# Spilled gate matrices laid out in DRAM by partition and group of four expert rows

## The reference

```
act  = einsum('thkd,td->thk', u_tab[experts], h)
coef = gates * gelu(act)
out  = einsum('thk,thkd->td', coef, v_tab[experts])
```

## Time and profile before

| | us |
|---|---|
| median of 3 runs | 2995.08 |
| lowest and highest run | 2994.76 and 2996.53 |
| span of the profiled execution, first to last instruction | 2994.5 |
| TensorE busy in that span | 2935.5 |

### The profile page before, as it was taken

The page is one execution under the profiler, slowest core; times in us unless marked ns, Lnnn a source line. Parts: engine busy times, 40 slices in busy tenths (PEclk is TensorE's granted clock), DMA queues, the critical chain, the costliest instruction groups (busy, mean ns, idle before and its releaser), DMA issues.

```text
span 2994.5 us, 49015 instructions
## 1 busy us (share of the span) xinstructions
PE 2935.5 (98%) x17798; PEld 2756.1 (92%) x17798; DVE 2529.9 (84%) x4848; ACT 1471.7 (49%) x2353; POOL 955.4 (32%) x709
## 2 busy tenths in 40 slices
PE   7999999999999999999999999999999999999998
PEld 4777799999999999999977778999999999999998
DVE  4667799989896899899886779998989868988988
ACT  3354234488884333333343532446888733333333
POOL 0000036545453333233300000655545433333331
PEclk9999999999999999999999999999999999999999
DMA  7425646799999999999931122569999899999996
GB/s 277 176 99 209 248 132 208 264 342 372 354 352 360 347 357 362 358 355 362 361 104 64 64 72 86 178 200 335 365 383 366 308 380 351 359 365 354 354 364 233
DMA packets 252363, 836.79 MB, mean 279 GB/s; under 512 B 24640, under 2 KB 57664, under 8 KB 241472
## 3 DMA queue, kind: packets, MB, share of 16 engines
q1 hardware_dynamic: 158336, 453.50, 42.5%
q0 software_dynamic: 89280, 348.17, 31.6%
q10 hardware_dynamic: 4608, 33.56, 2.7%
HBM read 751.24 MB, written 83.89 MB: 279 GB/s over the span
## 4 chain that ended last, share of the span: by engine, by line
PE 86%; DVE 5%; DMA 4%; ACT 2%; issue 1%; POOL 0%; SPq 0%; DVEq 0%; ACTq 0%; POOLq 0%
PE banks L998 41%; PE banks L1511 31%; PE banks L1479 5%; DMA w_raw<-wst 2%; PE banks L1319 2%; DVE w_lo L1552 1%; PE banks L1063 1%; PE banks L1014 1%; DMA ring<-u,gidx 1%; ACT w_hi L712 1%; PE banks L1402 1%; DMA pj<-adaw 1%; DVE vacc L2051 1%; PE banks L1493 0%; PE banks L1160 0%
## 5 line engine op out<-in xcount | busy, mean ns | idle before, releaser
L712 ACT ACTIVATE w_hi<-w_raw 128x1024 fp32r<-128x1024 f32 x596 | 631.7, 1060 | 813.1 <-PE banks L998 636.9
L1552 DVE TENSOR_TENSOR w_lo<-w_raw,w_hi 128x1024 fp32r<-128x1024 f32 x522 | 639.3, 1225 | 345.2 <-ACT w_hi L712 335.5
L998 PE MATMUL banks<-hH,w_hi 128*128 128x368 f32 (+1 forms) x2528 | 881.5, 349 | 5.5 <-ACT w_hi L712 2.4
L998 PE MATMUL banks<-hH,w_lo 128*128 128x368 f32 (+1 forms) x2528 | 861.1, 341 | 0.0
L998 PE MATMUL banks<-hL,w_hi 128*128 128x368 f32 (+1 forms) x2528 | 860.6, 340 | 0.0
L1511 PE MATMUL banks<-c_hi,w_hi 128*128 128x368 f32 x2048 | 675.8, 330 | 2.1 <-DVE w_lo L1552 2.1
L1511 PE MATMUL banks<-c_lo,w_hi 128*128 128x368 f32 x2048 | 674.3, 329 | 0.0
L1511 PE MATMUL banks<-c_hi,w_lo 128*128 128x368 f32 x2048 | 673.0, 329 | 0.0
L676 POOL DMA_INDIRECT ring<-u,gidx x288 | 420.9, 1461 | 451.6 <-DVE gact L2039 417.6
L676 POOL DMA_INDIRECT ring<-v,gidx x288 | 330.6, 1148 | 695.7 <-DVE vacc L2051 635.9
L998 PEld LDWEIGHTS banks<-hH,w_hi 128*128 128x128 f32 x2528 | 475.3, 188 | 50.5 <-issue 18.6
(11 more groups left out here) (323 smaller groups left out, 2966.3 us busy)
## 6 DMA issues: line engine op xcount, KB each, us to landing
w_raw<-wst SPq DMA_DIRECT2D x596, 512.0 KB
activations<-act_out SPq DMA_DIRECT2D x128, 368.0 KB
act_in<-activations SPq DMA_DIRECT2D x64, 736.0 KB
gate_matrices<-stage ACTq DMA_DIRECT2D x32, 1024.0 KB
gates<-gate_matrices SPq DMA_DIRECT2D x64, 512.0 KB
ada_buf<-adaw POOLq DMA_DIRECT2D x24, 1024.0 KB, 7.0
nrm<-adaw POOLq DMA_DIRECT2D x8, 1024.0 KB, 5.3
pj<-adaw POOLq DMA_DIRECT2D x7, 1024.0 KB, 7.1
```

The source lines that it names most:

```text
L712: nc.scalar.activation(w_hi[g % 2][:, :, :].rearrange("p a b -> p (a b)"), w_raw[:, g % RAWS, :], ACT.Copy).then_inc(s_wh, 1)
L998: last = mm(bank[s][:, 0:t.stop - t.start], a[s][:, k, :], b[:, k, t], start=(k == 0 and a is w_hi and b is hH), stop=(k == KT - 1 and a i ...
L1552: v.tensor_tensor(w_lo[g % 2][:, :, :].rearrange("p a b -> p (a b)"), w_raw[:, g % RAWS, :], w_hi[g % 2][:, :, :].rearrange("p a b -> p (a ...
```

## The change

The DRAM tensor `gate_matrices` had the order chunk, partition, row, token. It gets the order partition, group of four rows, chunk, row in the group, token. The same bytes are stored and loaded, by the same 32 stores and 64 loads, at the same places of each engine's program, behind the same waits. What differs is how long a run of neighbouring bytes in DRAM is for each partition.

- A load of a group's gates (512 KB) took for each partition four runs of 1 KB, one from each chunk, 4 MB apart, and the partitions lay 32 KB apart. It now takes one run of 4 KB, and the partitions lie 128 KB apart.
- A store of 32 rows of one chunk (1 MB) wrote for each partition one run of 8 KB. It now writes eight runs of 1 KB, 4 KB apart.

The tiles on chip keep their layout.

```diff
@@ load_gates, in the SyncE program
                 s = g % 2
                 sp.dma_start(gates[s][:, :, :, :],
-                             g_dram[:, :, g * GROUP:(g + 1) * GROUP, :].rearrange("c p b t -> p c b t")
+                             g_dram[:, g, :, :, :]
                              ).then_inc(s_gin[s], 16)
@@ stores of the gates, in the ScalarE program
                         e = slice(part * STORE_KEYS, (part + 1) * STORE_KEYS)
                         act.wait_ge(s_gv, l * QUADS + (c + 1) * CHUNK_QUADS + 2)
-                        act.dma_start(g_dram[c][:, e, :].rearrange("p e t -> p (e t)"),
-                                      stage[c % 2][:, e, :].rearrange("p e t -> p (e t)")).then_inc(s_gst[c % 2], 16)
+                        groups = slice(e.start // GROUP, e.stop // GROUP)
+                        act.dma_start(g_dram[:, groups, c, :, :].rearrange("p g b t -> p g (b t)"),
+                                      stage[c % 2][:, e, :].rearrange("p (g b) t -> p g (b t)", b=GROUP)
+                                      ).then_inc(s_gst[c % 2], 16)
@@ the tensor
-    g_dram = nc.dram_tensor("gate_matrices", (GSTORED, P, N_KEYS, GCHUNK), F32).ap()
+    g_dram = nc.dram_tensor("gate_matrices", (P, GROUPS, GSTORED, GROUP, GCHUNK), F32).ap()
```

## The result

The changed kernel takes 3034.0 us (median of 4 runs, 3031.02 to 3035.79) against 2994.92 us for the kernel before on the same chip: a ratio of 1.0128, 95% interval 1.0113 to 1.0142. It is slower by 39 us, where 2992.5 was predicted. The span of the profiled execution is 3034.1 us against 2994.5.

A forecast was written before the change was run, and what follows sets the result against it. TensorE was taken as the bound. Loads -2.6, issue 0 and stores 0 took 2995.1 us to a forecast of 2992.5 us, range 2989.5 to 3000.

The forecast's parts named there:

- What bounds the kernel: Beside gate loads and stores TensorE is the bound; only 3.9 and 1.3 us of its idle time can return.
- The loads: Before and in the V passes, late weight loads queued behind gate loads come earlier: -2.6 us, two thirds of 3.9.
- The cost of a small write: At the U pass's stores, a 1 KB write holds a DMA engine 46 ns, +0.47 us a store; effect taken as 0.
- the small writes fill the bursts: Rival at the four store bursts a layer: 2999 to 3010 us; chance 0.12 over 3001, 0.04 for 2997 to 3001.
- the pitch: Rival at the gate loads: partitions 128 KB apart double the time of 4 KB packets, 3040 us; chance 0.02.
- The 13% of room: In the stretch with stores, DMA slices between bursts were taken to have 13% free for 7.5 us more work a layer.
- The issue: ScalarE's issue of an eight-run store costs about 0.3 us more, 5 us a layer, hidden: 0, or 10 us uncovered.
- my signs of being wrong: From 640 to 890 us: q10's share over 28%, TensorE idle over 3 us; or store waits at a chunk's first quad.
- The cover: Beside the stores ScalarE is busy 210 of 250 us and TensorE does not wait for it, so longer issues cost 0.

The follow-up runs named there:

- the best kernels: Changed kernel with stores in pairs, 2991.89 us; as eight half stores, 2992.09; or every second row, 2991.64 and 2992.58 in two trials.
- the spaced runs: Changed kernel with its 1 KB stores issued further apart, such as every second row instead of every row: 2991.64 and 2992.58 us.
- the experiments' own form: Order of before and 1 KB-run loads, only stores cut: 2 KB runs 2993.67 us, 1 KB 3037.15, 512 B 3048.89.
- run 460: Not a follow-up run: the issue of a gate load in one run of bytes a partition takes 460 ns, against 466 in four.

## Why the prediction was wrong

**What bounds the kernel** held. TensorE was the bound, the idle time to be won was 5 us, and the best kernels won 2.6 to 4.3.

**The loads** are not refuted and not shown. The term was -2.6 us; alone they brought 1.5 us, which the interval does not tell from nothing. They were not where the change was decided.

**The cost of a small write** held to the digit. I took 46 ns and q10's share near 19%; it was 46 ns and 18.9%. The rival "the small writes fill the bursts" was priced on it and did not come about, as the spaced runs show with the same packets. My chance of 0.14 for slower stood on that rival and on the pitch, and neither was the mechanism. The 13% of room beside it were read from GB/s (365 of 420) where the DMA share stood at 0.97; nothing came to hang on that.

**The issue** is the step that failed: "From one run to four costs 0.14 us, so eight runs cost about 0.3 us more", "Cost **0**; if that cover were gone, 32 x 0.3 = 10 us". The miss was no bad luck: this term had no path to more than 10 us. Two readings in it were off. The number of runs hardly sets the plain price. The eight runs cost 366 ns against 326, the experiments' own form 520 ns with 4, 8 and 16 runs alike, and a load in one run 460 against 466 in four. And the row of 326/326/358 ns is the time of an issue that finds room. I read it as a price by the form of the transfer, and did not ask how many runs wait in ScalarE's queue at once. Four stores follow each other by a row (3.3 to 5.8 us), while in the changed kernel the packets of one take 3 to 15 us by their records in the trace. With more than some 76 runs ahead the third or fourth store is then an issue of 1.8 to 8.0 us. I had even listed in my favour that a small packet lets the other queues go first. If so, it makes q10 drain later: the second store of the first burst landed after 17 us, where it was 9. That the sharing does this was not tested by itself. What waits for q10 is not the landing but ScalarE itself, at the next issue. Of my signs of being wrong one came, TensorE's idle time from 640 to 890 us, 16.6 us where I had set 3; q10's share stayed under 28%, and no wait for stores appeared at a first quad.

**The cover** was read wrongly with it. ScalarE is busy 84% in that stretch, so 0.3 us fit beside TensorE, but its program is in order, with the one-hots for the next quads and `w_hi` behind the store. A held issue of 7.94 us became 5.4 us of TensorE. The Trainium skill, page "DMA: Bandwidth & Descriptors", section "Issuing engines are not separate DMA queues", says the time to initiate a DMA is usually small relative to the DMA itself. Here it is 0.37 us in the usual case and up to 7.96 us where stores crowd, so the trace shows the exception.

**What stays open** is the exact measure of the room. Some 75 to 95 runs ahead separate held from not held in nearly all issues, but not at one number for all three sizes, and two issues break it. The averages over the engines hide which engine lags, and how long a held issue lasts is not explained. Whether read or write runs count, or whether the queue of SyncE shares something, wasn't tried.

## What to carry to other kernels

A DMA issue is a price only as long as its queue has room. When a change cuts a transfer into more runs, count the runs that stand ahead of it in its queue at the tightest burst, and look at what stands behind the issue in that engine's program. If the total traffic is unchanged, spacing the issues can give all of the loss back: here one number, a store every second row instead of every row, was worth some 42 us (from 39 over before to 3 to 4 under). And a spacing has its own end, the reuse of the buffer that is stored.

## What the runs showed of the hardware

- The issue of a 1 MB store in 64 runs an engine took 0.37 us with up to 76 runs of earlier stores not landed, and 1.8 to 8.0 us with 83 to 113; ScalarE stood idle meanwhile (6.3 us before its next operation, at an issue of 7.94 us).
- A 1 KB write to DRAM held a DMA engine for 46 ns, as a 1 KB read did; 8 KB, 310 ns.
- TensorE's granted clock was 0.50 from 666.4 to 673.1 us, in and behind an idle stretch of 5.4 us, and as long behind the other four waits of 4.9 us and more; behind the waits of 0.8, 2.3 and 3.0 us it stayed at 1.00; TensorE's busy time grew by 10.9 us beside the 31.6 us of waiting.
